# PEER encoder layer on one core: after gather 301 the ring has six slots, and the seventh keeps head 7's query weights

## What is computed

```python
q = (xb @ wq).reshape(PEER_BLOCK, PEER_HEADS, 2, D_KEY_HALF)       # 8 heads, 2 x 128
s1 = jnp.einsum('thd,hnd->thn', q[:, :, 0], keys1)
s2 = jnp.einsum('thd,hnd->thn', q[:, :, 1], keys2)
v1, i1 = lax.top_k(s1, PEER_TOPK)
v2, i2 = lax.top_k(s2, PEER_TOPK)
...
top_s, sel = lax.top_k(cand, PEER_TOPK)                            # 16 experts per head
gate = jax.nn.softmax(top_s.astype(jnp.float32), axis=-1).astype(xb.dtype)
act = jax.nn.gelu(jnp.einsum('td,thkd->thk', xb, u_tab[eidx]))
return jnp.einsum('thk,thkd->td', gate * act, v_tab[eidx])
```

## Time and profile before

| | |
|---|---|
| median of 3 runs | 2945.81 us (2945.35 to 2950.26) |
| the profiled execution | 2945.65 us, its span 2943.8 us |
| busy: PE, DVE, ACT, POOL | 78%, 71%, 67%, 42% |
| DMA | 1205.73 MB, mean 410 GB/s |
| of it by gathers (queue 0) | 1107.36 MB |
| mean granted TensorE clock | 0.853 |

### The profile page before, as it was taken

One profiled execution on the slowest core, in us unless ns is written; L12 is line 12 of the kernel. 1 busy time (PEld: TensorE's weight loads), 2 busy tenths in 40 slices (PEclk: granted clock), 3 DMA queues, 4 the chain that ended last, 5 costly groups with the idle time before them and its releaser, 6 DMA issues.

```text
span 2943.8 us, 36236 instructions
## 1 busy us (share of the span) xinstructions
PE 2300.3 (78%) x12548; PEld 1804.2 (61%) x12548; DVE 2077.0 (71%) x5143; ACT 1967.8 (67%) x3670; POOL 1240.7 (42%) x1063
## 2 busy tenths in 40 slices
PE   9989898998777768888986887778766667666677
PEld 8878786665555556666665555555555555555555
DVE  3677788675688787777666555788868788865544
ACT  2477666777677677666667776777767666667663
POOL 0234334444334334433344344344454445455553
PEclk9999999999888878999996989898866656766669
DMA  8899999999999999999999999999999999999998
GB/s 340 318 403 404 420 408 411 412 420 420 420 419 417 412 410 404 421 421 419 418 418 404 419 420 421 412 420 418 411 419 410 420 420 416 403 414 416 422 421 361
DMA packets 182055, 1205.73 MB, mean 410 GB/s; under 512 B 21744, under 2 KB 27184, under 8 KB 43504
## 3 DMA queue, kind: packets, MB, share of 16 engines
q0 software_dynamic: 152368, 1107.36, 91.2%
q1 hardware_dynamic: 29264, 95.93, 8.3%
q10 hardware_dynamic: 240, 0.13, 0.0%
HBM read 1198.48 MB, written 4.86 MB: 409 GB/s over the span
## 4 chain that ended last, share of the span: by engine, by line
DMA 38%; DVE 24%; PE 22%; ACT 10%; issue 4%; POOL 1%; DVEq 0%; SPq 0%; ACTq 0%; POOLq 0%
DMA ring<-in_uv,idx 38%; DVE ring L2014 12%; PE expert_sum L1590 9%; ACT ring L1210 5%; PE x_ps L1371 2%; PE mm L1473 2%; ACT weights L1206 1%; POOL ring L950 1%; PE mm L1276 1%; DVE pairs_left L1819 1%; DVE pairs_left L1938 1%; ACT L1190 1%; ACT dots L1190 1%; PE expert_sum L1276 1%; PE x_ps L1276 1%
## 5 line engine op out<-in xcount | busy, mean ns | idle before, releaser
L950 POOL DMA_INDIRECT ring<-in_uv,idx x1054 | 1235.1, 1172 | 1683.8 <-PE expert_sum L1590 1464.1
L1590 PE MATMUL expert_sum<-ident_sb,ring 128*128 128x128 f32 x8192 | 1356.6, 322 | 594.5 <-ACT ring L1210 587.8
L2014 DVE CUSTOM_DVE_ANT_0 ring<-ring,xn 128x1024 f32<-128x1024 f32 x1056 | 1285.0, 1222 | 656.8 <-DMA ring<-in_uv,idx 646.8
L1590 PEld LDWEIGHTS expert_sum<-ident_sb,ring 128*128 128x128 f32 x8192 | 1130.2, 167 | 893.4 <-ACT ring L1210 827.6
L1210 ACT ACTIVATE ring<-ring,weights 128x1024 f32<-128x1024 f32 x1024 | 1176.2, 1149 | 33.3
L1190 ACT ACTIVATE dots<-dots 128x1 f32<-128x1 f32 x1056 | 211.5, 200 | 798.7 <-DVE dots L2014 792.2
L1206 ACT ACTIVATE weights<-dots,gate 128x1 f32<-128x1 f32 x1024 | 301.7, 295 | 37.1
L1473 PE MATMUL mm<-xn_in,stream 128*128 128x416 f32 (+1 forms) x500 | 198.3, 521 | 0.0
L1276 PE MATMUL mm<-stream,xn_in 128*128 128x256 f32 (+1 forms) x640 | 162.0, 387 | 0.0
L1276 PEld LDWEIGHTS mm<-stream,xn_in 128*128 128x128 f32 (+1 forms) x640 | 103.9, 177 | 21.4 <-issue 3.8
L1473 PEld LDWEIGHTS mm<-xn_in,stream 128*128 128x128 f32 x500 | 89.9, 200 | 39.6 <-issue 25.1
(11 more groups left out here) (397 smaller groups left out, 1955.6 us busy)
## 6 DMA issues: line engine op xcount, KB each, us to landing
stream<-in_wq SPq DMA_DIRECT2D x21, 1024.0 KB
ring<-in_uv,idx POOLq DMA_INDIRECT x1054
stream<-in_w_conv SPq DMA_DIRECT2D x16, 1024.0 KB
stream<-in_w_ret SPq DMA_DIRECT2D x16, 1024.0 KB
ring<-in_w_ret SPq DMA_DIRECT2D x6, 1024.0 KB, 12.4
x<-in_x SPq DMA_DIRECT2D x8, 512.0 KB, 10.0
out_y<-xn SPq DMA_DIRECT2D x8, 512.0 KB
stream<-in_w_out SPq DMA_DIRECT2D x3, 1024.0 KB
```

The lines of the kernel that those rows point to most:

```text
L950: pool.indirect_dma_start(ring[:, g % RING, :], None, uv, bass.IndirectOffsetOnAxis(ap=rows, axis=0)).then_inc(landed[g % RING], 16)
L1590: ins = pe.matmul(expert_sum[:, c * P:(c + 1) * P], ring[:, g % RING, D + c * P:D + (c + 1) * P], ident_sb[:, :], is_transpose=True, start ...
L2014: dve.tensor_tensor_reduce(u, u, xn[:, t % 2, :], 1.0, 0.0, ALU.mult, ALU.add, dots[:, g % RING:g % RING + 1]).then_inc(dotted, 1)
```

## The change

From gather 301 on (SMALL_RING = 43 * 7) gathers go round slots 0 to 5. Slot 6, last used by gather 300, receives head 7's query weights once, when 301 gathers have been freed, and the last pass of the second and of the third group reads them there. The two loads through the stream buffers fall away. Three helpers give a gather's slot, the lap of its slot and the gather before it in the same slot, and replace `g % RING`, `g // RING` and `g - RING` on POOL, ACT, PE and DVE.

```diff
+SMALL_RING = 43 * RING
+def slot_of(g):
+    return g % RING if g < SMALL_RING else (g - SMALL_RING) % (RING - 1)
+def lap_of(g):
+    return g // RING if g < SMALL_RING else SMALL_RING // RING + (g - SMALL_RING) // (RING - 1)
+def same_slot_before(g):
+    return g - RING if g < SMALL_RING + RING - 1 else g - RING + 1
...
-ON_CHIP = {n: p[1] for n, p in enumerate(PASSES) if p[2] == (0,) or p[2] == (1,) and p[1] in (2, 3)}
+ON_CHIP = {n: p[1] for n, p in enumerate(PASSES) if p[2] == (0,) or p[2] == (1,) and p[1] in (2, 3) or p[0] and p[1] == PH - 1}
...
+                yield SMALL_RING + 1
+                sp.wait_ge(slot_free, SMALL_RING)
+                sp.dma_start(ring[:, RING - 1, :].rearrange("p (b k n) -> p b k n", b=2, k=KC),
+                             wq[2 * PH - 2:2 * PH].rearrange("b p k n -> p b k n")).then_inc(kept_wq_in, 16)
...
-                    pool.wait_ge(slot_free, g - RING + 1)
+                    pool.wait_ge(slot_free, same_slot_before(g) + 1)
...
-                pool.indirect_dma_start(ring[:, g % RING, :], None, uv,
-                                        bass.IndirectOffsetOnAxis(ap=rows, axis=0)).then_inc(landed[g % RING], 16)
+                pool.indirect_dma_start(ring[:, slot_of(g), :], None, uv,
+                                        bass.IndirectOffsetOnAxis(ap=rows, axis=0)).then_inc(landed[slot_of(g)], 16)
...
-                    if m in ON_CHIP and h > 1:
+                    if m in ON_CHIP and j:
+                        pe.wait_ge(kept_wq_in, 16)
+                        weight = [chunks_of([ring[:, RING - 1, s * D:(s + 1) * D]]) for s in range(2)]
+                    elif m in ON_CHIP and h > 1:
...
-                dve.wait_ge(landed[g % RING], 16 * (g // RING + 1))
-                u = ring[:, g % RING, 0:D]
+                dve.wait_ge(landed[slot_of(g)], 16 * (lap_of(g) + 1))
+                u = ring[:, slot_of(g), 0:D]
```

More of the change, by code:

```diff
@@ L618, in layer_kernel @@
         held_conv_in, conv_rest_in, wq_rest_in = sem("held_conv_in"), sem("conv_rest_in"), sem("wq_rest_in")
-        third_wq_in, fourth_wq_in = sem("third_wq_in"), sem("fourth_wq_in")
+        third_wq_in, fourth_wq_in, kept_wq_in = sem("third_wq_in"), sem("fourth_wq_in"), sem("kept_wq_in")
         ret_in = [sem(f"ret_in{u}") for u in range(RING)]
@@ L935, in _ @@
                     pool.wait_ge(split_idx, 4)
-                    pool.indirect_dma_start(ring[:, g % RING, 0:D], None, uv.rearrange("n (h d) -> (n h) d", h=2),
+                    pool.indirect_dma_start(ring[:, slot_of(g), 0:D], None, uv.rearrange("n (h d) -> (n h) d", h=2),
                                             bass.IndirectOffsetOnAxis(ap=split_rows[:, 0, late:late + 1], axis=0)
-                                            ).then_inc(landed[g % RING], 16)
+                                            ).then_inc(landed[slot_of(g)], 16)
                     if late:
                         for i in range(2):
-                            pool.indirect_dma_start(ring[:, (g - 1) % RING, D + i * D // 2:D + (i + 1) * D // 2], None,
+                            pool.indirect_dma_start(ring[:, slot_of(g - 1), D + i * D // 2:D + (i + 1) * D // 2], None,
                                                     uv.rearrange("n (q d) -> (n q) d", q=4),
@@ L944, in _ @@
                                                     ).then_inc(last_v_in[i], 16)
-                        pool.indirect_dma_start(ring[:, g % RING, D:], None, uv.rearrange("n (h d) -> (n h) d", h=2),
+                        pool.indirect_dma_start(ring[:, slot_of(g), D:], None, uv.rearrange("n (h d) -> (n h) d", h=2),
                                                 bass.IndirectOffsetOnAxis(ap=split_rows[:, 1, late:late + 1], axis=0)
@@ L1182, in _ @@
                 t, k = tile_of(g)
-                d = dots[:, g % RING:g % RING + 1]
+                d = dots[:, slot_of(g):slot_of(g) + 1]
                 if t == SAMPLE and k == 0:
@@ L1204, in _ @@
                 act.wait_ge(gelu_done, g + 1)
-                w = weights[:, g % RING:g % RING + 1]
+                w = weights[:, slot_of(g):slot_of(g) + 1]
                 act.activation(w, d, ACT.Copy,
@@ L1208, in _ @@
                 act.wait_ge(weighed, g + 1)
-                v = ring[:, g % RING, D:2 * D]
+                v = ring[:, slot_of(g), D:2 * D]
                 act.activation(v, v, ACT.Copy, scale=w).then_inc(scaled, 1)
@@ L1579, in _ @@
                         pe.wait_ge(last_v_in[0], 16)
-                        spread_sum(spread[:, k % 3, :], P, ring[:, g % RING, D:], False, False, range(0, 2))
+                        spread_sum(spread[:, k % 3, :], P, ring[:, slot_of(g), D:], False, False, range(0, 2))
                         pe.wait_ge(last_v_in[1], 16)
-                        spread_sum(spread[:, k % 3, :], P, ring[:, g % RING, D:], False, False,
+                        spread_sum(spread[:, k % 3, :], P, ring[:, slot_of(g), D:], False, False,
                                    range(2, QUADS)).then_inc(slot_free, 1)
@@ L1586, in _ @@
                         pe.wait_ge(last_v_in[2], 16)
-                    spread_sum(spread[:, k % 3, :], P, ring[:, g % RING, D:], False, g + 1 == TOTAL).then_inc(slot_free, 1)
+                    spread_sum(spread[:, k % 3, :], P, ring[:, slot_of(g), D:], False, g + 1 == TOTAL).then_inc(slot_free, 1)
                     continue
                 for c in range(KC):
-                    ins = pe.matmul(expert_sum[:, c * P:(c + 1) * P], ring[:, g % RING, D + c * P:D + (c + 1) * P],
+                    ins = pe.matmul(expert_sum[:, c * P:(c + 1) * P], ring[:, slot_of(g), D + c * P:D + (c + 1) * P],
                                     ident_sb[:, :], is_transpose=True, start=False, stop=(g + 1 == end_of(t)),
@@ L2011, in _ @@
                         dve.wait_ge(xn_placed, t - 1)
-                dve.wait_ge(landed[g % RING], 16 * (g // RING + 1))
-                u = ring[:, g % RING, 0:D]
+                dve.wait_ge(landed[slot_of(g)], 16 * (lap_of(g) + 1))
+                u = ring[:, slot_of(g), 0:D]
                 dve.tensor_tensor_reduce(u, u, xn[:, t % 2, :], 1.0, 0.0, ALU.mult, ALU.add,
-                                         dots[:, g % RING:g % RING + 1]).then_inc(dotted, 1)
+                                         dots[:, slot_of(g):slot_of(g) + 1]).then_inc(dotted, 1)
                 advance(programs, g)
```

## The result

The changed kernel takes 2963.33 us (median of 6 runs, 2957.18 to 2969.75) against 2946.82 us of the kernel before (6 runs): ratio 1.0055, 95% interval 1.0044 to 1.0066, 16.5 us slower. The forecast was 2978, slower by 32; the sign and the range held, the size was twice what was measured.

The account below looks back on a forecast made before the run. The prediction took the DMA engines as the bound: +34.9 us for the lost slot at 14 stalls, -2.5 for one MB less, +32.4 on the profiled 2945.65, so 2978 us; range 2953 to 3005.

Parts of the forecast that it names:

- The bound: Whole kernel: its DMA engines set the pace, so bytes count, plus the time in which those engines lack work.
- Steps (a) to (d): One MB less traffic, -2.5 us; the kept load's wait on SP, PE's reads from the ring and slot arithmetic, 0 each.
- Step (e): Ring from gather 301 on: with six slots each draining stall costs one gather more, 14 x 2.5 us, +34.9 us.
- The landing time in the reserve: Gather from issue to landing: 6.1 us from the kernel's start, so hold-ups up to 6.1 (seven slots) or 3.6 (six) cost nothing.
- D: Rival: six slots short all the time, landing needing most of 12.2 us; at 10.2 us, 58 us more, 3036 us; chance 0.07.
- The number of stalls times 2.5 us: 960 to 2850 us: 14 stalls under 400 GB/s, each one gather of 2.5 us more, 34.9 us; range 17.4 to 70.
- unseen: Stalls between 3.6 and 6.1 us long, traceless in today's rate, would begin to cost at six slots; left out of +34.9.
- The same 14 stalls deeper: Changed profile's long stretch: the stalls already under 400 GB/s return deeper, with 30 to 40 such windows instead of 19.
- The Trainium skill's: One DMA transfer: 2.0 us plus bytes at 436 GB/s, 4.4 us here; slack 7.8 us now, 5.3 at six slots; not used.

## Why the prediction was right, and where its size was off

- **The bound** was right: the DMA engines set the pace. A run with 2 MB less is 4 us faster, and the slots taken from the ring cost time while the engines' busy times grow by 13 us at most in the changed kernel, none of them over 78% of its span.
- **Steps (a) to (d)** were right. The MB removed is worth about 2.2 us by the run without either load, 2.5 forecast. The kept load went out at 956.1 us (958 forecast), 85 us ahead of its first use, and nothing behind it on SP was late (the next load went out at 967.0 us, 968.0 before).
- **Step (e)**, that the seventh slot is reserve and that its loss costs DMA time, was right in kind: the run with six slots alone has the whole cost, and the reserve measured with held-up gathers falls by 2.8 us from seven slots to six, one gather's time. Its size went wrong in two terms, which partly cancelled.
- **The landing time in the reserve** was mis-sized. I took 6.1 us from the earlier trace rows, gathers with one other on its way. With five slots and 384 GB/s it takes 8.3 us; a way round of 5.3 + 8.3 = 13.6 us then leaves 17.4 - 13.6 = 3.8 us at seven slots and 1.3 at six. The hold-ups measured 3.9 and 1.1 to 1.4, not 6.1 and 3.6. The point in D's favour, that landings need more at full rate, was half true: with 8.3 instead of D's 10.2 the way round is one which six slots (14.9) just hold and five (12.4) don't. The row set against it, the gather issued at 1122.09 and used after 6.6 us, came right after a stall, when the queue was nearly as short as in the earlier trace rows. It could not speak for the full pace. A smaller reserve by itself would have made the change cost more than forecast.
- **The number of stalls times 2.5 us** was mis-sized the other way: 34.9 us forecast, 21.3 measured between the two profiled executions. I had taken every window under 400 GB/s for a stall that overruns seven slots. The run with eight slots still has 17 of them and loses 21.8 us, though its ring covers all but one of 706 ways from DVE to the next issue: price times count stood on windows most of which have another cause. How much of the 23.9 us at seven slots came from too small a ring is known only from the times, which an eighth slot did not change. Nor is it shown that the DMA engines had run dry in every such window, as I had argued: in the one at 1010 us the bytes fall by 9% and the busy share by 3%. The new loss comes in good part from delays that were within the reserve before, as at 1390 and 2310 us, the very ones that I had called unseen and left out. That the sum still came within a factor of two is in part luck: a reserve taken too large and a count of the wrong windows pulled in opposite directions.
- **What the changed profile would show**: 31 windows under 400 (30 to 40 forecast), quiet windows at 420 to 421, DVE's waits up by 33.4 us (some 30), mean 411 GB/s (409). "The same 14 stalls deeper" was wrong.
- **The Trainium skill's** fit (DMA: Bandwidth & Descriptors, Anatomy of one DMA), an estimate of 4.4 us for this size, is not borne out for a gather in a running queue: the shortest that DVE waited for in any profiled execution here took 5.4 us from issue to use, and the median at five slots is 8.6. Sized with that estimate, five slots would have 12.4 - (5.2 + 4.4) = 2.8 us to spare; the run with five slots lost 171 us.

## What to carry to other kernels

Where transfers are the bound, a ring of buffers is enough as long as slots x time per transfer exceeds the way round with the landing time measured at full pace, plus the longest delay of the engines that free the slots; past that a slot is worth nothing (eight against seven, until a longer delay was put in), one below it costs a little (six: 0.55% here), and the next one costs at every transfer (five: 5.8%). Holding an engine up at a few places, by two known lengths, measures that reserve in two runs; it is a safer reading than counting the windows in which the bandwidth is already low, since those may have another cause. Keeping data on chip in place of reloading it saves at most its transfer time, here 2 to 2.5 us per MB where the DMA is the limit and nothing where it isn't (the keys), and a ring slot is a dear place for it.

## What the runs showed of the hardware

- A gather of 1 MB took 5.7 and 6.1 us from issue to use with one other under way, and 7.3 at four slots and 8.3 at five in the ways round shown, where DVE waited for the DMA every time. The medians of the gathers that DVE waited for are 7.6, 8.6, 10.0, 12.5 and 15.0 us at four to eight slots.
- The landing semaphore of a gather gets 16 increments, and the trace has their times. From first to last they lie 1.9 us apart at five slots, 2.2 at six, 3.7 at seven and 6.0 at eight (medians after gather 310). That the increments stand for the 16 DMA engines, that these drift apart the deeper the queue is, and that this is why a landing needs 8.3 us at nearly full pace, is argued, not shown.
- In the 17 low windows of the run with eight slots the rate falls by 10% (378 GB/s against 420 in the others), the busy share of the DMA only by 4% (0.98 against 1.01): the median packet of 8 KB takes 0.31 us, and 5.4% of them take over 0.45 us there (the longest 2.1), against 0.3% elsewhere. In the low windows of the run with six slots and five passes of hold-up, where the ring did run short, 6.6% are as long, so this does not tell the two causes apart.
- What takes the 21.8 us that are lost even with eight slots stays open. In the window at 1610 us of that run the issues of two gathers on POOL take 3.50 and 4.47 us instead of 0.94 (timeline), which would let the DMA run short with free slots at hand; it was not tried. It could explain few of the windows: only 4 of the 718 issues from 960 to 2850 us take 2 us or more, and 13 of the 17 windows have none of these in them or in the 8 us before.

```profile
1606.96 3.50 POOL L969 DMA_INDIRECT ring<-in_uv,idx  x1 [1.27 <-PE expert_sum L1609]
...
1613.26 4.47 POOL L969 DMA_INDIRECT ring<-in_uv,idx  x1 [0.30 <-issue]
```
